# Where the sixteen early units of the output projection stand: one per block of the differential mixer, or all behind its last block

## The reference

```python
xn = rms_norm(h, norm_mix);  proj = xn @ w_in            # q, k, v of both mixers
oa = sliding_window_sink_attention(qa, ka, va, ...)       # 8 heads of 64, width 512
ob = differential_attention(qb, kb, vb, ...)              # 4 heads, width 512, 128-query blocks
h = h + concatenate([oa, ob]) @ w_out                     # the output projection
h = h + gated_conv_ffn(rms_norm(h), ...)
h = h + sigmoid(rms_norm(h) @ w_ple_gate) * (p @ w_ple)
return rms_norm(h, norm_final)
```

## Time and profile before

| | |
|---|---|
| median of 3 runs | 1290.88 us |
| the profiled execution | 1291.0 us, of which the instructions span 1289.2 us |
| mean granted PE clock over the span | 0.987 |
| PE, DVE, ACT, POOL busy | 1217.1, 876.3, 519.7, 325.1 us |
| iterations 22 to 31 of the differential mixer | about 343 to 396.5 us of the span |
| iterations 32 to 35 | about 396.5 to 413 us |
| PE without work behind them | 13.3 us, to 426.5 us |

### The profile page before, as it was taken

The page is one execution under the profiler, slowest core; times in us unless marked ns, Lnnn a source line. Parts: engine busy times, 40 slices in busy tenths (PEclk is TensorE's granted clock), DMA queues, the critical chain, the costliest instruction groups (busy, mean ns, idle before and its releaser), DMA issues.

```text
span 1289.2 us, 16975 instructions
## 1 busy us (share of the span) xinstructions
PE 1217.1 (94%) x6103; PEld 996.7 (77%) x6103; DVE 876.3 (68%) x1466; ACT 519.7 (40%) x1042; POOL 325.1 (25%) x335
## 2 busy tenths in 40 slices
PE   4999999999686799999999999999999999999997
PEld 3997787787565687888888888888888768888885
DVE  3432776777776276877877777878678997863442
ACT  4321664665554133433333333333344334642321
POOL 0000000444454011333223233133126780000000
PEclk9999999999889899999999999999999999999999
DMA  6364233012912411333323333323397534620101
GB/s 202 77 99 87 50 83 83 30 42 74 264 51 49 148 49 66 90 99 109 96 82 123 101 103 99 99 89 116 138 321 272 164 104 137 196 81 25 41 33 49
DMA packets 128669, 136.08 MB, mean 106 GB/s; under 512 B 15570, under 2 KB 93130, under 8 KB 128522
## 3 DMA queue, kind: packets, MB, share of 16 engines
q1 hardware_dynamic: 128586, 135.00, 34.9%
HBM read 96.77 MB, written 37.22 MB: 104 GB/s over the span
## 4 chain that ended last, share of the span: by engine, by line
PE 57%; DVE 7%; issue 2%; DMA 1%; SPq 0%; ACT 0%; POOL 0%; POOLq 0%; DVEq 0%; ACTq 0%
PE ps L1680 56%; DVE wbuf L1180 4%; DVE more L1180 1%; DVE h L1606 1%; PE ps L1690 1%; DMA raw<-u_ops 1%; DMA raw<-in_w_out 1%; PE ps L1886 1%; SPq L479 0%; ACT wbuf L799 0%; DVE conv L1403 0%; PE ps L2040 0%; POOL stat L678 0%; DVE xs L1465 0%; DVE gel L1673 0%
## 5 line engine op out<-in xcount | busy, mean ns | idle before, releaser
L1680 PE MATMUL ps<-act_t,wbuf 128*128 128x512 f32 x1200 | 288.8, 396 | 2.9 <-DVE wbuf L1180 2.9
L1680 PEld LDWEIGHTS ps<-act_t,wbuf 128*128 128x128 f32 x1200 | 225.7, 188 | 57.5 <-issue 3.3
L1680 PE MATMUL ps<-wbuf 128*128 128x512 f32 x912 | 217.1, 392 | 2.1 <-DVE wbuf L1180 2.1
L1680 PEld LDWEIGHTS ps<-wbuf 128*128 128x128 f32 x912 | 170.1, 188 | 40.9 <-DVE wbuf L1180 4.1
L1680 PE MATMUL ps<-act_t,wq 128*128 128x512 f32 x624 | 155.7, 402 | 3.6 <-DVE wq L1182 2.8
L1680 PEld LDWEIGHTS ps<-act_t,wq 128*128 128x128 f32 x624 | 114.6, 188 | 33.4 <-issue 7.4
L1180 DVE TENSOR_TENSOR wbuf<-raw,wbuf 128x512 fp32r<-128x512 f32 (+1 forms) x107 | 105.1, 983 | 21.3 <-ACT wbuf L799 21.0
L678 POOL TENSOR_TENSOR stat<-stat 128x1 f32<-128x1 f32 x32 | 17.6, 551 | 360.6 <-DVE stat L1189 360.6
L799 ACT ACTIVATE wbuf<-raw 128x512 fp32r<-128x512 f32 (+1 forms) x107 | 69.3, 649 | 93.3 <-PE ps L1680 65.5
L1680 PE MATMUL ps<-hx,wbuf 128*128 128x512 f32 x408 | 96.2, 391 | 0.0
L1680 PEld LDWEIGHTS ps<-hx,wbuf 128*128 128x128 f32 x408 | 76.5, 188 | 16.6
(11 more groups left out here) (197 smaller groups left out, 2056.8 us busy)
## 6 DMA issues: line engine op xcount, KB each, us to landing
u_ops<-wbuf_f SPq DMA_DIRECT2D x77, 256.0 KB, 2.2
raw<-u_ops SPq DMA_DIRECT2D x77, 256.0 KB, 2.7
raw<-in_w_ffn_in SPq DMA_DIRECT2D x33, 512.0 KB, 3.9
g_ffn<-in_w_ffn_in SPq DMA_DIRECT2D x11, 512.0 KB, 4.1
act_f<-in_w_ffn_out SPq DMA_DIRECT2D x21, 256.0 KB, 3.8
w_raw<-in_w_in SPq DMA_DIRECT2D x10, 512.0 KB, 4.5
wbuf_f<-in_w_ffn_out SPq DMA_DIRECT2D x18, 256.0 KB, 6.9
x_in<-in_x SPq DMA_DIRECT2D x8, 512.0 KB, 3.7
```

Of the source, the lines that this page charges most:

```text
L1680: return nc.tensor.matmul(dst, lhs, rhs, start=start, stop=stop)
```

## The change

`C_FROM`, the first iteration with an early unit, goes from 22 to 32 (`NBS`), and the iterations from 32 on take five units each, not two. Before, iterations 22 to 31 had one unit each, 32 to 34 two each. After, iterations 32, 33 and 34 have five each and iteration 35 has the sixteenth. `c_bank` follows from `C_FROM`: before, units 0 to 10 use bank 0 and the others alternate; after, all alternate, and unit 1 is the one that waits for the last exponentials.

```diff
     C_ROWS = 2
-    C_FROM = 22
+    C_FROM = NBS
     VIA_DRAM = 2 * NT
 
     def c_units(n):
@@
         if n < NBS:
             return (n - C_FROM,)
-        first = NBS - C_FROM + 2 * (n - NBS)
-        return tuple(c for c in (first, first + 1) if c < 2 * NT)
+        first = NBS - C_FROM + 5 * (n - NBS)
+        return tuple(c for c in range(first, first + 5) if c < 2 * NT)
 
     def c_bank(c):
         return c % 2 if c > NBS - C_FROM else 0
```

## The result

The changed kernel took 1309.75 us (median of four, 1309.07 to 1311.17), beside 1291.1 for the kernel before (median of four): a ratio of 1.0146, interval 1.0128 to 1.0163. It is slower by 18.7 us; forecast were 16.6 (a time of 1307.5, range 1303 to 1312.5). The profiled execution took 1309.6 us with a span of 1307.8, 18.6 more than the 1289.2 of before.

What follows compares the result with a forecast made beforehand. The end of unit 15, which SP waits for, was taken to set the stretch, with a fixed chain behind it. 1291.0 + 14.4 (units behind the last block) + 2.2 (clock) = 1307.6, on the median 1307.5 us; range 1303 to 1312.5.

Steps and rivals of the forecast that it cites:

- The end of unit 15 sets the rest, 15.8 us behind it follow unchanged: Behind unit 15: SP waits for its end, then transfers, loads and splits take a fixed 15.8 us to `oproj`.
- Units and adds taken out of the blocks give nothing back: Iterations 22 to 31: ten units on PE and ten adds on DVE lie under waits for other engines, costed at 0.
- 14.4 us behind the last block: Iterations 32 to 35: ten added units and waits for adds make `c_done` complete 14.4 us later.
- up to 3.3 in the bounds: Head of iteration 32: slow units at the low clock, 0.7 us from the first two and 2.6 from the next two.
- 2.2 us for the clock in the blocks: Blocks 22 to 31 without units: PE's clock falls several times, costing 2.2 us, bounds 0 and 8.9 us.
- The place that was priced: Pv of block 22, which ACT waits for, with eight turnings in front: +2.2 us at the low clock.
- lengthened no block: Kernel before, 367 to 374 us: a clock fall of some 7 us cost nothing, since the blocks didn't wait for PE.
- an unchanged pace of blocks 27 to 31: Sign in the profile after: first exponentials of blocks 27 to 31 still 4.64, 5.27, 5.92, 6.57 us apart.
- The Trainium skill's rule: Ten blocks: half the throttled time is added, up to 26.7 us if throttled throughout, a time of some 1332.
- The hole absorbed nothing: Rival, hole before `oproj`: the 14.4 us eat the 13.3 us hole first, leaving 1294.3 us; chance 0.03.
- no block became faster: Rival, ten blocks: unit and add are on the ring, each block gives back up to 2.0 us, 1285.4; chance 0.02.
- the larger clock loss: Rival, blocks and iteration 32: clock falls meet every place where PE is waited for, 8.9 us, 1314 us; chance 0.13.

Runs made afterwards that it cites:

- work behind unit 15: Kernel before, with 60 matmuls that nobody reads on PE behind unit 15, in front of the rest of the projection: 1289.40 us, ratio 0.9987.
- the loads ahead: SP loads the last two rows of w_out in front of its wait for unit 15: changed kernel 1296.85 us, kernel before 1278.09 us.
- filler in place of the units: Changed kernel, with six matmuls that nobody reads put back in each of iterations 22 to 31: 1307.47 us, ratio to before 1.0121.
- the two-units-first kernel: Changed kernel, with the units behind the last block as 2, 6, 7 and 1, not 5, 5, 5 and 1: 1308.64 us.
- the better placing of the last six units: Kernel before, ten units left in the blocks, the remaining six as five and one, not two, two, two: 1289.78 us, ratio 0.9992.

## Why the prediction was right

- **The end of unit 15 sets the rest, 15.8 us behind it follow unchanged.** Right: 15.91, and between 15.5 and 16.0 in every kernel that keeps SP's order. Shown from both sides: work behind unit 15 costs nothing, and with the loads ahead the distance falls to about 3 us.
- **Units and adds taken out of the blocks give nothing back.** Right at the full clock. With filler in place of the units and no adds A to B is 52.30 (52.33 before), so the adds were worth nothing. Where the units were missing and the clock was full, the pace is the old one too: blocks 29 to 30 of the changed kernel, with the clock at 1.00 from 384 to 388, took 5.91 us (5.92 before).
- **14.4 us behind the last block.** Measured 16.62. The terms held: 13.1 for ten units at 1.31, a first wait for adds (1.92 us; worked out at 1.86, from 399.1 to 400.96), a second of 0.26 (at 0.55). The clock aside, the stretch came out 0.6 us longer than the 14.4; back to back a unit took (7.03 - 1.64) / 4 = 1.35 us by the rows at 420.77 and 427.67, which makes 0.4 of it. The term that was sized wrong is the clock in this stretch: I had it at 0 in the sum and up to 3.3 in the bounds; it was 1.64 in this execution. With the clock full B to C was 30.77, 14.95 more than before.
- **2.2 us for the clock in the blocks.** The blocks lost 2.64, but that the sum came so near is in part luck. The place that was priced gave 1.17 in this execution (exponentials of 24 to 25 took 6.43, not 5.26 us), as the pv slowed to 2.98 us while the turnings in front of it were still fast. In other runs, among them the two-units-first kernel, both were slow and the step took 7.45 us, the 2.2 of the forecast. The rest came from slow scores in other blocks, although the text had said that a fall "lengthened no block" and had named an unchanged pace of blocks 27 to 31 as a sign of being right: 22 to 23 took 6.96, not 6.55 us, 27 to 28 took 5.09, not 4.64, 28 to 29 took 5.65, not 5.27. At 30 to 31 (6.76, not 6.57) it was a slow pv again, which ACT waited for. So that sign failed, though the mechanism behind it (at full clock units and adds cost the blocks nothing) did not. The low stretch at 367 to 374 of the kernel before had covered a unit and turnings, but the scores at 374.09 of that trace ran at full clock; slow scores do hold DVE up, by 0.37 us in front of the logits of block 28. I had priced that only in the upper bound.
- **The Trainium skill's rule** ("TensorE: Matmul & The Clock Gate", section "HAM oscillation — how this bites in real kernels") has it that bursts with waits between them are throttled, and the trace of the changed kernel agrees: by the mean clock of the windows of 4 us between 344 and 400, PE was at 1.2 GHz for about 32 us, and for about 7 in the kernel before. By the page's half of the throttled time the estimate of the loss would be 16 us, and there the trace differs: the blocks lost 2.64.
- **The rivals.** The hole absorbed nothing (C to D unchanged), no block became faster by more than 0.01 us, and of the larger clock loss about 4.3 us (2.64 + 1.64) of 8.9 came. The forecast of 16.6 and the 18.7 measured differ by the 0.4 and the 1.6 that the clock took beyond its term and the 0.6 of the units and their waits, less some 0.6 us in which the start and the end of the execution differ.

## What to carry to other kernels

Work is not free to move because the engine has a hole behind it: look at what opens and closes the hole. Here it hangs on the end of the moved work, through a queue, so work in front of the signal counts in full and the same work behind it not at all. And look at what else stands in that queue: two loads that needed nothing of the wait were behind it, and moving them ahead gave 13 us, ten times the 1.3 us of the better placing of the last six units.

## What the runs showed of the hardware that was not expected

- Six matmuls per block, read by nobody, were worth 2.3 us, and 60 in front of a restart 1.7 us. With the first the granted clock fell once in the blocks from 22 to 31, at 368 to 374, and was at 1.00 in the others; with the second it was at 1.00 all through the hole and behind it.
- The clock also falls in blocks that have their units, and then a unit is in the way. In the kernel before with loads ahead it was at 0.50 in 376 to 380; the unit took 2.93 us there, DVE waited 1.14 us to add it, and blocks 28 to 29 took 6.39 us, not 5.27. The timeline of that kernel:

```profile
375.71 2.93 PE L1679 MATMUL ps<-act_t 128*128 128x512 f32 x6
...
379.10 0.69 DVE L1319 TENSOR_TENSOR h<-ps,h 128x512 f32<-128x512 f32 x1 [1.14 <-PE ps L1679]
```

- Where the clock falls differs from run to run of nearly the same instructions (units 2 to 4 at 0.50 in the changed kernel, at 1.00 behind nearly the same wait in the one with loads ahead). This alone moved B to C by 1.6 us, so a difference of that size between two single executions says little here.
